# A chain of fp32-split matrix products: turning the state-space input matrices by products with the identity, and the low activations as the last sweep of a first chunk

## The reference, cut to what matters

```
ab = exp(lam * dt)                       # one complex decay per state
bb = (ab - 1) / lam * b                  # the input matrix, 64 states x 16 channels
s[t] = ab * s[t-1] + bb @ u[t]           # per group
y[t] = Re(c @ s[t]) + d * u[t]
out = gelu(y) @ w_glu, gated
```

## Time and profile before

| | |
|---|---|
| median of 3 runs | 3015.19 us (3011.47 to 3016.48) |
| the profiled execution, its own time | 3012.33 us |
| its span, first to last instruction | 3010.6 us |
| mean granted TensorE clock | 0.988 |
| PE busy | 2929.1 us (97% of the span) |
| DVE busy | 1650.2 us (55%) |
| ACT busy | 1411.4 us (47%) |
| PE busy, PE clock in the stage `s_in`, 2472 to 2496 us | 23.89 of 24.00 us, clock 1.00 |
| the same, 2531 to 2583 us | 52.00 of 52.00 us, clock 0.95 |
| the same, 2583 to 2623 us | 40.00 of 40.00 us, clock 0.94 |

### The profile page before, as it was taken

One profiled execution on the slowest core, in us unless ns is written; L12 is line 12 of the kernel. 1 busy time (PEld: TensorE's weight loads), 2 busy tenths in 40 slices (PEclk: granted clock), 3 DMA queues, 4 the chain that ended last, 5 costly groups with the idle time before them and its releaser, 6 DMA issues.

```text
span 3010.6 us, 36311 instructions
## 1 busy us (share of the span) xinstructions
PE 2929.1 (97%) x14538; PEld 2429.7 (81%) x14538; DVE 1650.2 (55%) x2038; ACT 1411.4 (47%) x1802; POOL 25.3 (1%) x43
## 2 busy tenths in 40 slices
PE   8999999999999999999999999999999999999998
PEld 7878877788888888878887788888888877787876
DVE  5775655554544454564445555444445575776545
ACT  5544376544444444454446454444444454354444
POOL 0000000000000000000000000000000001000000
PEclk9999999999999999999999999999999998999999
DMA  6532245565555565555552555555555644344543
GB/s 234 181 126 85 85 153 186 170 196 194 183 194 194 184 195 191 187 181 185 192 185 85 202 181 189 189 193 190 192 194 181 200 150 137 116 155 155 193 160 126
DMA packets 255842, 516.77 MB, mean 172 GB/s; under 512 B 8528, under 2 KB 8752, under 8 KB 254688
## 3 DMA queue, kind: packets, MB, share of 16 engines
q1 hardware_dynamic: 252896, 501.61, 50.5%
q0 software_dynamic: 2816, 13.33, 1.3%
HBM read 511.76 MB, written 2.10 MB: 171 GB/s over the span
## 4 chain that ended last, share of the span: by engine, by line
PE 92%; DVE 4%; ACT 3%; issue 1%; DMA 0%; SPq 0%; ACTq 0%; DVEq 0%
PE acc L474 83%; PE side L670 2%; ACT ar L1118 1%; DVE ar L1806 1%; DVE wlo L1818 1%; PE side L536 1%; PE side L781 1%; PE side L927 1%; PE side L565 1%; ACT whi L1129 0%; DVE ar L1809 0%; PE side L929 0%; DMA raw<-in_ev_w_in 0%; ACT L1118 0%; PE side L938 0%
## 5 line engine op out<-in xcount | busy, mean ns | idle before, releaser
L1818 DVE TENSOR_TENSOR wlo<-raw,whi 128x1024 fp32r<-128x1024 f32 x948 | 1154.5, 1224 | 1176.8 <-ACT whi L1129 1176.2
L1129 ACT ACTIVATE whi<-raw 128x1024 fp32r<-128x1024 f32 x948 | 997.8, 1060 | 1211.4 <-PE acc L474 1210.7
L474 PE MATMUL acc<-whi,xh 128*128 128x512 f32 x3008 | 825.8, 397 | 7.7 <-ACT whi L1129 4.2
L474 PE MATMUL acc<-whi,xl 128*128 128x512 f32 x3008 | 809.9, 391 | 0.0
L474 PE MATMUL acc<-wlo,xh 128*128 128x512 f32 x3008 | 808.1, 391 | 0.1
L474 PEld LDWEIGHTS acc<-whi,xl 128*128 128x128 f32 x3008 | 568.4, 189 | 120.6
L474 PEld LDWEIGHTS acc<-wlo,xh 128*128 128x128 f32 x3008 | 567.6, 189 | 120.0 <-DVE wlo L1818 0.5
L474 PEld LDWEIGHTS acc<-whi,xh 128*128 128x128 f32 x3008 | 558.7, 189 | 120.2 <-DVE xl L1809 5.0
L474 PE MATMUL acc<-whi,hTh 128*128 128x512 f32 x784 | 211.6, 392 | 5.8 <-DVE ar L1806 3.1
L474 PE MATMUL acc<-whi,hTl 128*128 128x512 f32 x784 | 210.5, 390 | 0.0
L474 PE MATMUL acc<-wlo,hTh 128*128 128x512 f32 x784 | 210.3, 390 | 0.1
(11 more groups left out here) (261 smaller groups left out, 1260.1 us busy)
## 6 DMA issues: line engine op xcount, KB each, us to landing
raw<-in_ffn_w_gate SPq DMA_DIRECT2D x88, 1024.0 KB, 5.2
raw<-in_ffn_w_up SPq DMA_DIRECT2D x88, 1024.0 KB, 5.1
raw<-in_ffn_w_down SPq DMA_DIRECT2D x88, 1024.0 KB, 5.0
raw<-in_ev_w_in SPq DMA_DIRECT2D x56, 1024.0 KB, 5.1
raw<-in_od_w_in SPq DMA_DIRECT2D x48, 1024.0 KB, 5.1
raw<-in_w_in SPq DMA_DIRECT2D x32, 1024.0 KB, 5.4
raw<-in_ev_w_out SPq DMA_DIRECT2D x16, 1024.0 KB, 5.0
raw<-in_od_w_out SPq DMA_DIRECT2D x16, 1024.0 KB, 5.0
```

The source lines that it names most:

```text
L474: mm = pe.matmul(acc[2 * pair + t][:], x[:, k0 + j, t * P:t * P + P], w[:, ring, j], start=start and j == 0, stop=stop and j == 1)
L1129: act.activation(whi[:, place % RING], raw_granule(place), ACT.Copy).then_inc(S("hi_done"), 1)
L1818: dve.tensor_tensor(wlo[:, place % RING], raw_granule(place), whi[:, place % RING].bitcast(F32), ALU.subtract).then_inc(S("lo_done"), 1)
```

## The change

Two edits, both in PE's program alone:

1. In `turn_b` the pieces with `g` = 0 are turned by a product with the identity as well. The instruction has the same operands and the same place in the order.
2. In the first chunk of the nine layers named above, the order of the sweeps is `xh` by `whi`, `xh` by `wlo`, `xl` by `whi`. Before the first sweep PE now waits for `xh` of round j, before the second for `wlo`, before the third for `xl` of round j. All other chunks keep their order.

```
-            def granule(g, ring, pair, lhs_h, lhs_l, k0, first, last):
+            def granule(g, ring, pair, lhs_h, lhs_l, k0, first, last, low=None):
...
                 pe.wait_ge(S("hi_done"), g + 1)
                 sweep(lhs_h, whi, start=first)
-                sweep(lhs_l, whi)
-                pe.wait_ge(S("lo_done"), g + 1)
-                sweep(lhs_h, wlo, stop=last).then_inc(S("used"), 1)
+                if low is None:
+                    sweep(lhs_l, whi)
+                    pe.wait_ge(S("lo_done"), g + 1)
+                    sweep(lhs_h, wlo, stop=last).then_inc(S("used"), 1)
+                else:
+                    pe.wait_ge(S("lo_done"), g + 1)
+                    sweep(lhs_h, wlo)
+                    pe.wait_ge(S("xl_done"), low)
+                    sweep(lhs_l, whi, stop=last).then_inc(S("used"), 1)
...
-            def wait_features(name, n=8):
-                pe.wait_ge(S("xl_done"), 2 * (8 * TOF[name] + n))
-
             def features_use(name, src=None):
-
                 def use(c, j):
                     if c == 0:
                         if src is not None and j < 3:
                             to_features(name, src, (range(4), range(4, 6), range(6, 8))[j])
-                        wait_features(name, j + 1)
+                        pe.wait_ge(S("xh_done"), 2 * (8 * TOF[name] + j + 1))
+                        return 2 * (8 * TOF[name] + j + 1)
                 return use
...
-                            if g:
-                                mm = pe.matmul(b[half(g), o:o + 64], x, one, start=True, stop=True)
-                            else:
-                                pe.transpose(b[half(g), o:o + 64], x, one)
+                            mm = pe.matmul(b[half(g), o:o + 64], x, one, start=True, stop=True)
```

More of the change, by code:

```diff
@@ L497, in granules @@
                             aside(c, j)
-                        if first_use:
-                            first_use(c, j)
+                        low = first_use(c, j) if first_use else None
                         if j == 0:
@@ L503, in granules @@
                         g = gran(name, c, j)
-                        granule(g, g % RING, pair, lhs_h, lhs_l, 2 * j, j == 0, j == per - 1)
+                        granule(g, g % RING, pair, lhs_h, lhs_l, 2 * j, j == 0, j == per - 1, low)
                         yield
@@ L799, in block_of @@
                                     pe.wait_ge(S("hm_done" if m else "sg_done"), 2 * n0 + 2 * i)
-                            if first and m == 0 and name[3] == "a":
-                                features_use(name, h)(0, j)
-                            granule(i * 16 + (g0 + 8 * m + j), j % RING, m, xh, xl, 2 * j, j == 0, j == 7)
+                            low = features_use(name, h)(0, j) if first and m == 0 and name[3] == "a" else None
+                            granule(i * 16 + (g0 + 8 * m + j), j % RING, m, xh, xl, 2 * j, j == 0, j == 7, low)
                 block_of(0, True)
```

## The result

| | before | after |
|---|---|---|
| median, us | 3014.34 (3011.47 to 3016.48, 4 runs) | 2980.14 (2979.80 to 2980.97, 4 runs) |
| profiled execution, us | 3012.33 | 2980.04 |
| its span, us | 3010.6 | 2978.3 |
| its mean granted clock | 0.988 | 0.993 |

The changed kernel takes 0.9887 of the time before, 95% interval 0.9876 to 0.9899: faster by 34 us. Foretold were 2980 us, range 2974 to 2992. The sum foretold between the profiled executions was -35.3 us; it came out as -32.3.

A forecast was written before the change was run, and what follows sets the result against it. PE was taken as the bound, 92% of the span. The terms -22.4 (turned pieces), -10.8 (clock) and -2.1 (sweep order) sum to -35.3 us, taking the median from 3015.19 to 2979.9, say 2980 us; range 2974 to 2992.

The forecast's parts named there:

- Edit 1, the price: Eight `turn_b` calls on PE, all by products, take 8.6 us instead of 31.0: -22.4 us.
- The reason given for the 0.26 us product: In `turn_b`, a product costs 0.26 us between two transposes because these have the array to themselves; without transposes, a quarter.
- Rival 3: At the eight `turn_b`: a product costs 0.26 us whatever stands beside it, so the median becomes 3018.9; 4%.
- Edit 1, the clock: Half-speed granules behind `turn_b` (g8, g9, g11, g30, g32) and a slowed `kernel_base` return to full speed: -10.8 us.
- stretches of small products alone do not bring it: Products without transposes bring no clock fall: 3.84 us of `kernel_base` and sixteen products of `inputs` precede full-speed sweeps.
- Rival 1: Clock still falls behind the turned products; g8, g11, g30, g32 stay slow: 2990.7, or between; 16%.
- The clock of positions 8 to 11: Sign to look for in `s_in`: the granted clock there becomes 1.00, from 0.69.
- Edit 2: New order of sweeps in first chunks: -0.64 - 0.31 - 1.92 + 0.79 = -2.1 us.
- `ev_out` and `od_out`: Idle time before granule 0, ended by DVE's `xl`, goes: 0.64 and 0.31 us.
- `s_out`: Two sweeps fit into PE's 2.51 us idle time before granule 0, which ends 1.92 us sooner.
- `s_in`: `wlo` is wanted a sweep earlier, so g7 starts 0.79 us later; up to 0.3 for `up0a`, `od_in`, `up1a` together.
- The cover: At positions 8 to 11, DVE's lead keeps its splits ahead of the shortened PE work, by 6 us.

The follow-up runs named there:

- grouped_mixed: Changed kernel, but each `turn_b` call does its eight g = 0 pieces by transposes first, then its eight g = 1 pieces by products; 2988.93 us (one run).
- full_products: Changed kernel with the 128x128 pieces in `turn` of `s_in` turned by products with the identity instead of transposes; 2983.65 us (one run).
- turn_only: Kernel before with only the `turn_b` pieces all turned by products, old order of sweeps; 2986.39 us, 0.9903 of before.
- twice: Changed kernel with each product of `turn_b` issued twice, the second over the first; 2982.71 us (one run).
- acc_first: Changed kernel with VectorE's last reads of the two gate accumulators made before the two products with `sgs`; 2978.58 us, 0.9882 of before.
- base_at_10: Changed kernel with PE's `kernel_base(0)` one granule later, at position 10 instead of 9; 2981.58 us, 0.9891 of before.
- first_granule: Changed kernel with the new order of sweeps only in granule 0 of the first chunks, old order in granules 1 to 7; 2978.49 us, 0.9885 of before.
- both_orders: Changed kernel with both first_granule's order of sweeps and acc_first's earlier accumulator reads; 2977.86 us, 0.9881 of before.

## Why the prediction was right, and where it was off

**Edit 1, the price: right.** -22.4 foretold, -22.6 measured. `inputs` was the right row to go by: single calls take 1.08 us, as it does. The reason given for the 0.26 us product was incomplete. It put the cost on a transpose that has the array to itself; what costs is each change of kind, near 0.13 us, and the transpose carries it too, 0.17 us instead of 0.07 (`grouped_mixed`). For sixteen products both reasons give the same number, so the price could be right without the whole cause. It also doesn't say that a part of the price was clock: the 3.5 us inside the double calls.

**Rival 3 and the rule beside it.** Away from transposes the product costs 0.063 where the halves alternate and 0.104 to 0.134 where they are grouped, never 0.26; rival 3 is out. What the Trainium skill says in Perfetto Trace Analysis, Optimizing Tensor Performance, Transposes, that a logical transpose is better done as a transpose, is borne out where a whole group is of one kind and of full size: 0.106 against 0.22 us a piece (`full_products`). Its reason, the skipped arithmetic, no run here tests. For 64x64 pieces a transpose in a group on one half, 0.07, is ahead of a product there and level with a product on alternating halves, 0.063; and mixing is worse than either.

**Edit 1, the clock: the mechanism right, the term too large.** -10.8 foretold, -9.3 measured. The step that failed is that "stretches of small products alone do not bring it". The 3.84 us of `kernel_base` at position 27 had no fall behind them; `kernel_base(0)` had one behind it in both profiles of the changed kernel, and the second `kernel_base` in `turn_only`. One row without a fall was taken for a rule. For `turn_b` itself it did hold: no products of `turn_b` were followed by a slow first sweep, in `twice` not even 3.93 us of them. Rival 1 came true for one granule of five. The clock of positions 8 to 11, foretold as 1.00, was 0.91. The kernel before also shows that the old calls did not always bring a fall. The one at position 26, 3.43 us of transposes and products, ends at 2586.35 and has a full-speed sweep behind it:

```profile
2586.35 1.19 PE L474 MATMUL acc<-whi,xh 128*128 128x512 f32 x4
```

**Edit 2: -2.1 foretold, -1.7 measured.** The sum is near because misses of both signs meet in it:
- `ev_out` and `od_out` gave 0.88 and 0.57, not 0.64 and 0.31. From the transposes' start to granule 0 it was 2.54 and 2.22 us before, and is 1.66 in both: the idle time in brackets starts at a modelled end of the records and was 0.2 to 0.3 too small as a price, in both.
- `s_out` gave 1.31, not 1.92. Late behind `xl` was the accumulator, read by VectorE until 2763.3 (`acc_first`). The prediction didn't ask what is late next.
- `s_in` cost 0.85, against 0.79, and granule 3 of `up0a` and of `up1a` 0.09 each, within the bound of 0.3 for the three layers named.

**The clock elsewhere: +1.3**, no term of the sum. This, edit 1's missing 1.3 (33.2 foretold, 31.9 measured) and edit 2's 0.4 are the 3 us between -35.3 and -32.3. The medians hid it: before's profiled execution lay 2 to 3 us under the median of its runs, after's at it.

**The cover.** g11 and g12 found their splits, as foretold: PE is busy all 18.1 us of positions 8 to 11, and DVE is now busy for 14.92 of them.

**What stays open.** Why the clock falls behind one `kernel_base` and not behind another: `twice` with more small work in front has no fall, `base_at_10` with more granules in front has one, and `first_granule`, the same work 0.8 us earlier, has it behind the second `kernel_base` and not the first. `both_orders`, with the same edit in `s_in`, does just the same, though counted from the start of the span its `turn_b` stands where the changed kernel has it (2495.30 and 2495.34); `acc_first`, which leaves `s_in` alone, keeps the fall of the changed kernel. No run here shows what decides. Nor does a run tell why the clock fell behind some of the old calls of `turn_b` and not behind others: each of these traces is a single execution.

## What to carry to other kernels

Do not alternate transposes and products on TensorE: group each kind, or use one kind throughout, and let neighbouring quarter-size products lie on different halves of the array. When a row gives a price for a mixture, don't divide it into the prices of its parts; find each part standing alone. And before a wait's time is booked as gained, list what else the same instruction needs, a free accumulator among it, and when each is ready.

## What the runs showed of the chip

- Alternating fp32 transposes and products of 64x64 pieces took 3.43 us for sixteen, the same sixteen grouped 1.63, sixteen products alternating between the halves 1.01 to 1.08, sixteen products grouped by half 1.67 to 1.83.
- Side work of some 4 us and idle time of 2.7 to 3.1 us (3.12 us before the sweep at 2731.7, 2.71 before the one at 2866 in the changed kernel) are sometimes followed by TensorE at half its clock for two or three sweeps (records of 1.91 us instead of 1.07), about 1.6 us a time. In two executions of the changed kernel the places were the same but for one. In several programs whose edit shifted work by a microsecond, falls stood elsewhere, so a difference of 1.6 us, or twice that, says nothing of the edit until the trace has been read.
